# Pages two with each of eight w_ada pieces, and a compression in sixteen parts, at the start of a hybrid decoder step

## What is computed

```
def adaln(c, w_ada, b_ada):                      # w_ada (2048, 6*2048): six chunks of 2048 columns
    m = jax.nn.silu(c) @ w_ada + b_ada
    return m.reshape(c.shape[0], 6, D_MODEL)

def modulate(x, shift, scale, g):                # chunk 0 is the shift, chunk 1 the scale
    return rms_norm(x, g) * (1.0 + scale[:, None, :]) + shift[:, None, :]

def compressed_kv(kv_rows, cmp_pe, w_cmp, g_k):  # 32 rows at a stride of 16, K and V, 4 groups
    blk = kv_rows[:, idx] + jnp.swapaxes(cmp_pe, 0, 1)
    comp = jnp.einsum('bnlcgd,cglde->bncge', blk, w_cmp)
...
    h = modulate(x, mod[:, 0], mod[:, 1], g_norm1)
    q, kvc, kvs, kvw, gates, u = mix_inputs(h, w_in, g_qnorm, g_knorm)   # h @ w_in
    full_c = jnp.concatenate([cache_kv_cmp[page_table]..., kvc], axis=1) # 16 cached pages of 128 rows
    kc, vc, pos_c = compressed_kv(full_c, cmp_pe, w_cmp, g_knorm[0])
```

## Time and profile before

| | |
|---|---|
| median of three timed runs | 2469.77 us |
| the profiled execution, and its span | 2463.28 us, 2461.3 us |
| TensorE busy, VectorE busy | 1272.7 us, 1762.7 us |
| DMA moved | 944.54 MB, mean 384 GB/s |
| start of the w_in stage (line 1080) | 153.64 us |

### The profile page before, as it was taken

The page is one execution under the profiler, slowest core; times in us unless marked ns, Lnnn a source line. Parts: engine busy times, 40 slices in busy tenths (PEclk is TensorE's granted clock), DMA queues, the critical chain, the costliest instruction groups (busy, mean ns, idle before and its releaser), DMA issues.

```text
span 2461.3 us, 18706 instructions
## 1 busy us (share of the span) xinstructions
PE 1272.7 (52%) x6783; PEld 703.7 (29%) x6785; DVE 1762.7 (72%) x2269; ACT 215.2 (9%) x561; POOL 1183.0 (48%) x686
## 2 busy tenths in 40 slices
PE   6799989898924541778959840000045555100000
PEld 3343434653404331654427800000012222000000
DVE  1020021497579988986667579999999997999897
ACT  3110032100011221210000110000000000000000
POOL 1000000032247545763315127788866766787884
PEclk8899989899965665558968955555577677555555
DMA  9979999699999989999999899999999999999997
GB/s 317 377 311 422 408 383 235 225 407 422 423 402 375 411 329 414 411 393 392 418 368 364 325 399 396 360 423 422 422 414 411 408 416 408 412 422 407 379 422 298
DMA packets 156678, 944.54 MB, mean 384 GB/s; under 512 B 18028, under 2 KB 31924, under 8 KB 52511
## 3 DMA queue, kind: packets, MB, share of 16 engines
q0 software_dynamic: 94784, 682.66, 68.1%
q1 hardware_dynamic: 61807, 260.74, 28.5%
HBM read 937.36 MB, written 10.26 MB: 385 GB/s over the span
## 4 chain that ended last, share of the span: by engine, by line
PE 29%; DMA 23%; DVE 21%; POOL 15%; issue 9%; ACT 2%; SPq 1%; POOLq 0%; DVEq 0%; ACTq 0%
DMA arena<-in_peer_u,arena 11%; POOL arena L672 9%; DVE arena L1989 8%; DMA arena<-in_peer_v,arena 6%; POOL arena L684 6%; PE PS L1454 3%; DVE arena L2012 3%; PE PS L1432 3%; DMA arena<-in_w_ada 3%; PE PS L1477 3%; PE PS L971 3%; PE PS L1172 2%; PE PS L1080 2%; DMA arena<-in_w_out 2%; DVE arena L2042 2%
## 5 line engine op out<-in xcount | busy, mean ns | idle before, releaser
L1989 DVE CUSTOM_DVE_ANT_0 arena<-arena 128x2048 f32<-128x2048 f32 x256 | 581.5, 2288 | 107.9 <-DMA arena<-in_peer_u,arena 106.1
L672 POOL DMA_INDIRECT arena<-in_peer_u,arena x256 | 455.8, 1780 | 415.9 <-DVE arena L1989 264.9
L2012 DVE SCALAR_TENSOR_TENSOR arena<-arena 128x2048 f32<-128x2048 f32 x226 | 531.0, 2350 | 108.8 <-DMA arena<-in_peer_v,arena 103.9
L672 POOL DMA_INDIRECT arena<-in_peer_v,arena x256 | 433.8, 1695 | 347.4 <-DVE arena L2012 219.5
L1477 PE MATMUL PS<-arena 128*128 128x512 f32 x240 | 174.8, 897 | 454.9 <-DMA arena<-in_peer_v,arena 448.9
L1477 PEld LDWEIGHTS PS<-arena 128*128 128x128 f32 x240 | 67.4, 295 | 563.1 <-issue 556.3
L1483 PE MATMUL PS<-arena 128*64 128x512 f32 x8 | 5.7, 873 | 346.4 <-DVEq L2055 346.4
L2045 DVE SCALAR_TENSOR_TENSOR arena<-arena 128x2048 f32<-128x2048 f32 x64 | 150.5, 2352 | 10.7 <-DMA arena<-in_peer_v,arena 5.3
L684 POOL DMA_INDIRECT arena<-in_peer_v,arena x64 | 134.8, 2105 | 35.2 <-issue 19.2
L971 PE MATMUL PS<-arena 128*32 128x512 f32 x768 | 117.0, 709 | 66.7 <-DMA arena<-in_w_ada 63.4
L2042 DVE CUSTOM_DVE_ANT_0 arena<-arena 128x2048 f32<-128x2048 f32 x64 | 144.9, 2291 | 8.5 <-DMA arena<-in_peer_u,arena 6.6
(11 more groups left out here) (341 smaller groups left out, 1872.9 us busy)
## 6 DMA issues: line engine op xcount, KB each, us to landing
arena<-in_w_ada SPq DMA_DIRECT2D x96, 1024.0 KB, 13.6
arena<-in_w_in SPq DMA_DIRECT2D x32, 1048.0 KB, 12.4
arena<-in_peer_wq SPq DMA_DIRECT2D x32, 1024.0 KB, 11.4
arena<-in_w_in SPq DMA_DIRECT2D x32, 768.0 KB, 12.3
arena<-in_w_out SPq DMA_DIRECT2D x24, 1024.0 KB, 26.2
arena<-in_w_out SPq DMA_DIRECT2D x16, 512.0 KB, 25.0
arena<-in_peer_u,arena POOLq DMA_INDIRECT x320, 13.8
arena<-in_peer_v,arena POOLq DMA_INDIRECT x320, 10.9
```

What stands on the lines that cost most here:

```text
L672: pool.indirect_dma_start(out=rows_ring[:, k % NROW, :], out_offset=None, in_=tables[kind], in_offset=bass.IndirectOffsetOnAxis(ap=ids[:, ...
L1989: V.tensor_tensor_reduce(out=buf, in0=buf, in1=h2(t), scale=1.0, scalar=0.0, op0=ALU.mult, op1=ALU.add, accum_out=dots[:, t, r:r + 1]).the ...
L2012: V.scalar_tensor_tensor(out=acc[t], in0=rows_ring[:, k % NROW, :], scalar=dots[:, t, r:r + 1], in1=acc[t], op0=ALU.mult, op1=ALU.add).the ...
```

## The change

Four things change. `cmp_pages(m0)` now issues two pages.

- SP: instead of pages 0-3, pieces 6-9, first compression weights, pages 4-7, pieces 10-13, pages 8-11, pieces 14-17, pages 12-15, second compression weights, pieces 18-31, it issues eight rounds of two pages and one piece (6 to 13); the first compression weights stand behind pages 6 and 7, the second behind pages 12 and 13; then pieces 14 to 31.
- TensorE: pieces 4 and 5 move from ahead of x's transposes to behind them. Then eight rounds of two pages and one piece, and pieces 14 and 15.
- TensorE: the compression goes in 16 parts of 16 matmuls (trace count), a piece of chunk 1 behind each. No piece of chunk 1 stands before the compression any more (there were four).
- ScalarE: all 16 page copies stand ahead of the copy of chunk 0.

```
-                for m in range(m0, m0 + 4):
+                for m in range(m0, m0 + 2):
...
-            cmp_pages(0)
-            load(6, 10)
-            cmp_weights(0)
-            cmp_pages(4)
-            load(10, 14)
-            cmp_pages(8)
-            load(14, 18)
-            cmp_pages(12)
-            cmp_weights(1)
-            load(18, n_start)
+            for i in range(8):
+                cmp_pages(2 * i)
+                if i in (3, 6):
+                    cmp_weights(i // 6)
+                load(6 + i, 7 + i)
+            load(14, n_start)
...
-            ada(0, 4, 6)
             pe.wait_ge(s_xn, 3)
...
-            pages(0, 4)
-            ada(0, 6, 10)
-            pages(4, 8)
-            ada(0, 10, 14)
-            pages(8, 12)
+            ada(0, 4, 6)
+            for i in range(8):
+                pages(2 * i, 2 * i + 2)
+                ada(0, 6 + i, 7 + i)
             ada(0, 14, 16)
-            ada(1, 0, 2)
-            pages(12, 16)
-            ada(1, 2, 4)
             pe.wait_ge(s_ctc, 16)
             pe.wait_ge(s_hA, NK // 2)
             pe.wait_ge(s_hD, NK // 2)
-            pe.wait_ge(s_wc[0], 16)
-            compress_sample(0, 0)
-            ada(1, 4, 7)
-            compress_sample(0, 1).then_inc(s_cmp, 1)
-            ada(1, 7, 10)
-            pe.wait_ge(s_adaC, 1)
-            mod1(0)
-            pe.wait_ge(s_wc[1], 16)
-            compress_sample(1, 0)
-            ada(1, 10, 13)
-            compress_sample(1, 1).then_inc(s_cmp, 1)
-            ada(1, 13, 16)
+            for i in range(16):
+                c, gp, q = i // 8, i // 4 % 2, i % 4
+                pe.wait_ge(s_wc[c], 16)
+                last = compress_sample(c, gp, range(4 * q, 4 * q + 4))
+                if i % 8 == 7:
+                    last.then_inc(s_cmp, 1)
+                ada(1, i, i + 1)
+                if i == 3:
+                    pe.wait_ge(s_adaC, 1)
+                    mod1(0)
             pe.wait_ge(s_adaC, 2)
             mod1(1).then_inc(s_m1, 1)
```

More of the change, by code:

```diff
@@ L719, in ct_out @@
                 A(CT[:, :, m // 2, (m % 2) * 64:(m % 2 + 1) * 64], PS[:, 2 + m % 4, :].rearrange("p (a b) -> p a b", a=8), copy).then_inc(s_ctc, 1)
-            for m in range(12):
+            for m in range(16):
                 ct_out(m)
             chunk_out(0)
-            for m in range(12, 16):
-                ct_out(m)
             chunk_out(1)
@@ L1020, in pages, with compress @@
                     turn_pairs(2 + m % 4, 0, cpage[:, m % 4], 128).then_inc(s_ct, 1)
-            def compress(bank, c, gp, src, n, step_to):
-                for l in range(CMP_BLOCK // 2):
+            def compress(bank, c, gp, src, n, step_to, steps=range(CMP_BLOCK // 2)):
+                for l in steps:
                     for gi in range(2):
@@ L1028, in compress, with compress_sample @@
                 return last
-            def compress_sample(c, gp):
-                return compress(c, c, gp, lambda k, s: CT[:, k, :, s], NS_C, CMP_STRIDE * (NC_ - 1))
+            def compress_sample(c, gp, steps):
+                return compress(c, c, gp, lambda k, s: CT[:, k, :, s], NS_C, CMP_STRIDE * (NC_ - 1), steps)
             def compress_prompt(c):
```

## The result

Eight runs of each on one chip: the changed kernel 2480.97 us median (2474.27 to 2485.60), the kernel before 2464.38 us (2461.93 to 2473.71). The ratio is 1.0053, with a 95% interval from 1.0035 to 1.0072, so 13 us slower, 9 to 18. I forecast 2479 us and 9.4 us slower. The profiled execution has a span of 2483.7 us.

What follows compares the result with a forecast made beforehand. No engine was taken as the bound throughout, but TensorE as setting the end of the first 154 us. Chunk 1 ending 10.4 us later, 9.4 coming through, on 2469.8 gave 2479 us, range 2465 to 2491.

Steps and rivals of the forecast that it cites:

- the first dry spell: DMA engines before page 4: nothing left in the queue from 43.6 to 57 us, dry for 13 us.
- TensorE's pace behind it: Chunk 1's steps: 3.1 us each on TensorE against 2.49 for a piece's transfer, so TensorE sets the pace.
- its own signs: Signs to look for in the new profile: first compression part at 105 to 109 us, line 1080 at 162 to 166.
- Part 1: SP's order up to page 4: page 4 issued at about 55 us, DMA dry for 13 us before its data.
- Part 2: Page 4 to the end of chunk 0: 46.8 us of transfers plus 1.5; compression starts at 106.5 us.
- the forecast's prices: Transfer times used in the sums: a piece 2.49 us, a page 0.62, one set of compression weights 9.7.
- Part 3: Compression in sixteen parts: four more pieces 3.6 us, 12 more changes 6.7; chunk 1 ends at 158.6 us, 10.4 later.
- Part 4: Later cost: line 1080 starts at 164.1 us; between 8 and 10.4 us come through, 9.4 taken.
- (a): Rival: the parts cost nothing and the dry spell is shorter; 2472 us, chance 0.14.
- (b): Rival: TensorE's clock falls in chunk 1, each piece 0.87 us more, chunk 1 24 us later; 2493 us, chance 0.22.
- (c): Rival: the spreading works, with page 4 not late, and chunk 1 ends 7.6 us earlier; 2462 us, chance 0.07.
- (d): Rival: a later DMA stretch absorbs the delay and 0 to 3 us remain; 2471 us, chance 0.07.

Runs made afterwards that it cites:

- e1: Changed kernel's TensorE order with SP's old list of pages, pieces and weights: ratio 1.0006 to the kernel before.
- e10: Changed kernel with the first compression weights behind piece 7, ahead of SP's wait, and the second behind piece 12: ratio 1.0019 to the kernel before.
- e2: Changed kernel with its compression in four parts again, four pieces of chunk 1 behind each: ratio 1.0041 to the kernel before.
- e6: Changed kernel with pieces 4 and 5 put back ahead of x's transposes: ratio 1.0047 to the kernel before.
- e8: Changed kernel reading the compression weights as 128 rows of 16 KB instead of 256-byte pieces: ratio 1.0009 to the kernel before.
- e5: Kernel before with only its compression cut into 16 parts, its 12 pieces of chunk 1 set between them: ratio 1.0010 to the kernel before.
- e12: Changed kernel with first weights ahead of SP's wait, second behind piece 17, four parts, and pieces 4 and 5 ahead of x's transposes: ratio 0.9994 to the kernel before.
- e11: Changed kernel with the first compression weights ahead of SP's wait and the second behind piece 17: ratio 1.0024 to the kernel before.
- e4: Kernel before with only the first half of the compression moved ahead of piece 18 on TensorE: ratio 0.9982 to the kernel before.

## Why the prediction was right, and where it was off

It had the sign and, within the interval, the size (9.4 us against 13, 9 to 18), and the first dry spell and TensorE's pace behind it came as it said. That 2479 lies so near the measured 2480.97 is partly luck: it was counted from a median of 2469.77 us, and the runs of the kernel before in this comparison had 2464.38. The start times missed its own signs: the compression at 115.7 (105 to 109 was said) and the w_in stage (line 1080 before, 1067 now) at 170.6 (162 to 166). By its own steps, in which 4.3 and 4.9 us too little stand against 2.8 too much:

- **Part 1, the dry spell: right, and larger.** Forecast from 43.6 to 57 us with page 4 at 55; measured 44 to 60 with page 4 at 59.3. Of the 4.3 us, 2.6 are a later start of x's transposes (39.59 instead of 36.98), which is how that execution ran: in the runs in four parts and with weights first, in which TensorE's list is the same up to there, they started at 35.2 and 38.6, with page 4 at 55.0 and 58.5. From x's start to page 4 it was 19.7 to 19.8 us in all three, where the forecast had 18.0. Of that, 1.38 us are the wait for VectorE's subkey copies, which I had not named: pieces 4 and 5 had covered them. What the spell costs is shown from two sides: with SP's old list it is gone and so is the loss (`e1`), and with the first weights ahead of SP's wait 0.34% comes back (`e10`). Both runs also take the first hold off the path, by the estimate below some 1 us.
- **Part 2, from page 4 to the compression: mis-sized.** I took 51.5 us; it was 56.4, and 56.1 and 56.3 in `e2` and `e6`, so this is no chance of one execution. I added 1.5 us for SP's issues and page buffers and did not see that an issue behind the weights holds SP for 11 us. The trace of before shows it: the issue at 83.58 lasts 12.69 us, and its chain has 8.25 us of SP issuing line 423 at 88.01; I read past both. But the hold is by estimate the smaller part of the miss. The weights' transfers were in the sum, and the DMA engines work on them while SP is held; with long rows the forecast's prices give 51.5 - 9.4 = 42.1 us and `e8` took 45.0. So about 3 us are missing with no hold at all, and some 2 us come with the holds, where the engines run short until SP has sent the next pages. Where the 3 us lie was not tested.
- **Part 3, sixteen parts: too large.** Four more pieces on TensorE and the changes were to add 10.3 us; from the compression's start to the end of chunk 1 (165.0) it was 49.3 us, against 41.8 before: 7.5. By the steps of `e5`, a change there and back costs 0.18 to 0.25 us and not 0.56. I had read the step between weight loads (0.105 us) as the step of the matmuls; two lengths of part, 16 and 64, give 0.109 us a matmul and 0.11 to 0.12 us for the end.
- **Part 4: what comes through was not measured closely enough.** I took off 1 us for the waits for w_ada pieces behind 320 us. In the changed kernel's profile these waits are longer, 14.0 us (window 340 to 382) against 9.7, and the output projection starts at 386.0 instead of 366.2, 19.8 us later, so this profile shows nothing absorbed. The ratio says 13 us, 9 to 18, for a w_in stage that starts 17.0 us later, or 14.4 without the late start of x's transposes, and both lie in that interval. Before's profiled execution (2463.28) is near the lower end of its runs, this one (2485.6) is the slowest of its eight.

```profile
PEld PS L965 <- DMA arena<-in_w_ada: 14.0, 7, 2.5
```

Of the rivals, (a) was half right: the parts cost little, but the dry spell was longer and not shorter. (b) did not come: from 115 to 152 us the clock is 0.92 of 2.4 GHz on average, one piece behind `mod1` takes 1.94 us, all others about 1.06. (c), no dry spell, needed more than the changed order gives; `e10` to `e12` come nearest to it, and only `e12`, with pieces 4 and 5 and four parts put back, is level with before. (d) is out: it left 0 to 3 us, and the interval begins at 9. The 0.28 for slower by over 0.5% was on the low side for 0.53.

What stays open: how the 12.1 us of `e8` split between transfer and hold beyond the working above, where the other 3 us of Part 2 lie, how much of the delay is absorbed later, and why `e11` and `e12` are slower in their runs than their start times say.

## What to carry to other kernels

Before a transfer is moved behind a wait on its issuing queue, add up what is in flight when that wait begins: the old order had some 15 us more of transfers issued ahead of a 19.5 us wait by what looked like clumsy grouping, and that was its merit. A transfer in short pieces held its queue here until it had nearly landed, so what stands next in the queue should be something that is not needed before. Look for where the engine waits before spreading its work: TensorE idled at 92 to 101 us, and work moved there (`e4`) gave 0.18%, where work cut into parts gave nothing.

## What the runs showed of the hardware

- SP's next DMA issue behind 2.1 MB in 256-byte pieces did not end before those had nearly landed: in all 17 such issues over 1.8 us, in 11 profiles, it ended 2.0 to 2.9 us before the landing. Its length followed from that, from 1.85 us behind a long wait to 9.9 to 13.2 us where SP came to it soon behind the weights and 19.92 and 20.53 us where they stood behind four pieces (`e11`, `e12`); the kernel before has 12.69. Behind the same bytes in 16 KB rows it was 0.43 us.
- Those 256-byte pieces ran at 213 to 224 GB/s, w_ada's rows at 422. Issued from ScalarE's queue beside a full SP queue, one such transfer took 57.9 us to land; from SP's own it took 13.0 to 25.6 in the other kernels with short pieces.
- TensorE ran at 1.2 GHz from 44 to 54 us in the kernel before and in the changed one while it was busy all the time, with x's transposes above all (10.00 of 10.00 us; in the changed kernel 0.50 in the same window); from 57 to 65 us, in the page transposes and pieces behind, the changed kernel's clock was 1.00. A row that is busy all the time did not by itself mean the higher clock here.
